# Norms between stages: gain on the rows, root in the turning diagonal, shift added in PSUM, splits of 512 columns, weight splits behind

## The reference

```
layers 0, 1:   x = layer_norm(ALPHA * x + mixer(x), g, b)
               x = layer_norm(ALPHA * x + conv_ffn(x), g, b)
layers 2, 3:   x = x + rmsnorm(mixer(rmsnorm(x, g0)), g1)
               x = x + rmsnorm(ffn(rmsnorm(x, g2)), g3)

layer_norm:    (x - mean) * rsqrt(var + 1e-5) * g + b      rows of 1024
rmsnorm:       x * rsqrt(mean(x*x) + 1e-6) * g
```

## Time and profile before

| | |
|---|---|
| median of 3 executions | 1635.89 us (1635.73 to 1636.53) |
| the profiled execution | 1639.12 us, span 1637.8 us |
| PE busy | 1476.4 us (90%), mean granted clock 0.936 |
| DVE busy | 989.1 us (60%) |
| ACT busy | 771.2 us (47%) |
| POOL busy | 348.8 us (21%) |
| DMA | 242.53 MB, 148 GB/s on average |

### The profile page before, as it was taken

How to read it: one execution, slowest core, us unless ns; L and a number is a source line. 1 busy time by engine, 2 the same in 40 slices (tenths; PEclk the granted TensorE clock), 3 DMA queues, 4 the chain that set the end, 5 groups by cost and what they waited for, 6 DMA issues and landing times.

```text
span 1637.8 us, 24046 instructions
## 1 busy us (share of the span) xinstructions
PE 1476.4 (90%) x9862; PEld 1318.7 (81%) x9862; DVE 989.1 (60%) x1721; ACT 771.2 (47%) x1168; POOL 348.8 (21%) x278
## 2 busy tenths in 40 slices
PE   7989987999989879999799989999897757989998
PEld 6888767999877769998666779999697755789997
DVE  5366447666638366676346265566579996265655
ACT  4343435455442255454444465444565553364443
POOL 0267132000177530001732410000100041500000
PEclk8999997999987979999899999999998976999999
DMA  7543223555344325654312335654442211335552
GB/s 267 223 167 116 103 77 129 184 206 190 141 148 155 129 103 185 227 180 155 134 73 91 114 118 183 215 180 155 180 155 104 104 53 64 129 136 199 193 184 74
DMA packets 37101, 242.53 MB, mean 148 GB/s; under 512 B 3928, under 2 KB 6272, under 8 KB 9472
## 3 DMA queue, kind: packets, MB, share of 16 engines
q1 hardware_dynamic: 36992, 241.00, 40.9%
HBM read 236.27 MB, written 4.72 MB: 147 GB/s over the span
## 4 chain that ended last, share of the span: by engine, by line
PE 74%; DVE 12%; ACT 7%; POOL 5%; issue 2%; DMA 0%; SPq 0%; ACTq 0%; DVEq 0%; POOLq 0%
PE ps L328 23%; PE ps L295 14%; PE ps L296 13%; PE ps L297 13%; POOL wlo L245 4%; DVE wlo L252 2%; ACT whi L237 2%; DVE gb L1938 1%; PE ps L1591 1%; PE ps L835 1%; PE ps L1605 1%; PE ps L426 1%; ACT gb L1847 1%; DVE ar L1975 1%; ACT XS L460 1%
## 5 line engine op out<-in xcount | busy, mean ns | idle before, releaser
L295 PE MATMUL ps<-XS,whi 128*128 128x256 f32 x2088 | 607.2, 291 | 28.5 <-DVE XS L480 18.1
L296 PE MATMUL ps<-XS,whi 128*128 128x256 f32 x2088 | 602.2, 288 | 0.0
L297 PE MATMUL ps<-XS,wlo 128*128 128x256 f32 x2088 | 601.6, 288 | 0.0
L252 DVE TENSOR_TENSOR wlo<-raw,whi 128x2048 fp32r<-128x2048 f32 x160 | 368.8, 2306 | 170.8 <-ACT whi L237 170.8
L237 ACT ACTIVATE whi<-raw 128x2048 fp32r<-128x2048 f32 x212 | 403.7, 1906 | 144.3 <-PE ps L328 132.1
L245 POOL TENSOR_TENSOR wlo<-raw,whi 128x512 fp32r<-128x512 f32 x206 | 275.3, 1369 | 827.2 <-ACT whi L237 827.2
L295 PEld LDWEIGHTS ps<-XS,whi 128*128 128x128 f32 x2088 | 412.9, 198 | 35.2 <-issue 24.6
L296 PEld LDWEIGHTS ps<-XS,whi 128*128 128x128 f32 x2088 | 412.6, 198 | 1.6 <-issue 0.2
L297 PEld LDWEIGHTS ps<-XS,wlo 128*128 128x128 f32 x2088 | 411.8, 197 | 0.0
L328 PE MATMUL ps<-whi,MS 128*128 128x512 f32 x1088 | 312.9, 393 | 12.1 <-POOL wlo L245 11.5
L328 PEld LDWEIGHTS ps<-whi,MS 128*128 128x128 f32 x1088 | 202.2, 189 | 55.2 <-POOL wlo L245 13.1
(11 more groups left out here) (264 smaller groups left out, 1590.7 us busy)
## 6 DMA issues: line engine op xcount, KB each, us to landing
raw<-in_up SPq DMA_DIRECT2D x88, 1024.0 KB, 4.8
raw<-in_down SPq DMA_DIRECT2D x44, 1024.0 KB, 4.8
raw<-in_hg_t SPq DMA_DIRECT2D x16, 1024.0 KB, 4.8
raw<-in_od_t SPq DMA_DIRECT2D x8, 1024.0 KB, 4.8
raw<-in_ev_a SPq DMA_DIRECT2D x7, 1024.0 KB, 5.1
raw<-in_wa_o SPq DMA_DIRECT2D x6, 1024.0 KB, 4.8
raw<-in_hg_o SPq DMA_DIRECT2D x6, 1024.0 KB, 4.8
raw<-in_mem_k SPq DMA_DIRECT2D x4, 1024.0 KB, 7.8
```

What stands on the lines that cost most here:

```text
L252: ve.tensor_tensor(lo[:, 0:w], r[:, 0:w], hi[:, 0:w].bitcast(F32), ALU.subtract).then_inc(w_lo_v)
L295: pe.matmul(d, hi[:, c], S[:, k, 0:256], start=(k == 0), stop=False)
L296: pe.matmul(d, hi[:, c], S[:, k, 256:512], start=False, stop=False)
L297: last = pe.matmul(d, lo[:, c], S[:, k, 0:256], start=False, stop=(k == 7))
```

## The change

- Norms 0 to 2: DVE multiplies the centred rows by the gain row in natural order (two operations of 512 columns, before the root is needed). The turn is an f32 matmul with a diagonal `dm` that holds the root. Ahead of each of its blocks stands a matmul with one row of contraction that writes the shift into PSUM (shift row against a row of ones), onto which the turn adds.
- Norms 3 to 6: DVE multiplies the new rows by the gain of the coming norm (`gp`, loaded by a new DMA from a DRAM copy that PE, ACT and SP make of the gain columns at norm 0), and these are turned; the order of the residual sum changes so that the multiplication by gb comes before the root.
- A turned bank holds four blocks: banks 4 and 5 for tt = 0, banks 2 and 3 (the accumulators just read) for tt = 1. ACT copies 512 columns a time to the high part, DVE subtracts 512 columns a time for the low part, of both row tiles. POOL splits none.
- The weight splits of tile `LAST[n] + 2` stand behind both row tiles on ACT and on DVE.
- The rows in natural order are made by DVE: `layer_rows_dve`, for norms 0 and 2 in the FFN at j = 2 and 4, for norm 1 at the start of the odd stage, for norm 3 in the norm. POOL has none left.
- SP no longer waits for the norm before it loads for the next stage, but for the last activations of the stage before. The squares on ACT go to the arena instead of yb. Two buffers of the even stage (QA, CN) share the place of QI and KI.

```diff
         def norm_pe(n):
+            if n == 0:
+                pe.transpose(bank[7][0:32, 0:128], pc[:, PC["rg"][0]:PC["rg"][1]], ident).then_inc(g_tp.up())
             for tt in range(2):
...
+                for q in range(2):
+                    o = turn_bank(tt, q)
+                    pe.wait_ge(ly.sem, 4 * n + 2 * tt + q + 1)
+                    pe.wait_ge(dg.sem, 2 * n + tt + 1)
+                    if n < 3:
+                        pe.wait_ge(d_gb, 16 * (n + 1))
+                    for i in range(4):
+                        k = 4 * q + i
+                        d = o[:, 128 * i:128 * i + 128]
                         if n < 3:
...
+                            pe.matmul(d, gb[0:1, 1, 128 * k:128 * k + 128], C("ones", 1)[:, 0:128], start=True, stop=False)
+                        last = pe.matmul(d, yb[:, tt, 128 * k:128 * k + 128], dm[:, tt, :], start=(n >= 3), stop=True)
                     last.then_inc(tp.up())
...
         def xs_act(n, tt):
...
+            for q in range(2):
+                hi, lo, bv = xs_views(tt, q)
+                ac.wait_ge(tp.sem, 4 * n + 2 * tt + q + 1)
+                ac.activation(hi, bv, ACT.Copy).then_inc(xh.up())
+
+        def xs_dve(n, tt):
+            for q in range(2):
+                hi, lo, bv = xs_views(tt, q)
+                ve.wait_ge(xh.sem, 4 * n + 2 * tt + q + 1)
+                ve.tensor_tensor(lo, bv, hi.bitcast(F32), ALU.subtract).then_inc((xs1 if tt else xs0).up())
...
             root_dve(st[:, o + 14:o + 15], st[:, o + 13:o + 14], 1.0, LN_EPS)
-            ve.tensor_scalar(yb[:, tt, :], yb[:, tt, :], st[:, o + 12:o + 13], st[:, o + 14:o + 15],
-                             ALU.subtract, ALU.mult).then_inc(ly.up())
+            ve.wait_ge(d_gb, 16 * (n + 1))
+            for h in range(2):
+                c = half_rows(h)
+                ins = ve.scalar_tensor_tensor(yb[:, tt, c], yb[:, tt, c], st[:, o + 12:o + 13], gb[:, 0, c], ALU.subtract,
+                                              ALU.mult)
+                ins.then_inc(ly.up() if n < 3 else dv.up())
+            meanwhile()
+            root_ready()
+
+        def diagonal_dve(tt, r):
+            ve.tensor_scalar(dm[:, tt, :], ident, r, None, ALU.mult).then_inc(dg.up())
+
+        def layer_rows_dve(n, tt):
+
+            o = 32 * tt
+            for h in range(2):
+                c = half_rows(h)
...
+                ve.scalar_tensor_tensor(xn[:, tt, c], yb[:, tt, c], st[:, o + 14:o + 15], gb[:, 1, c], ALU.mult,
+                                        ALU.add).then_inc(xr.up())
...
+        def residual_dve(n, tt):
+
+
+            def gained(h):
+                c = half_rows(h)
+                ve.tensor_tensor(yb[:, tt, c], accs[tt][h][:, :], gb[:, 0, c], ALU.mult).then_inc(dv.up())
+
+            ve.wait_ge(d_gb, 16 * (n + 1))
+            ve.wait_ge(sq.sem, got["sq"] + 1)
+            gained(0)
+            mean_square_dve(tt, 22)
+            gained(1)
+            root_ready()
+            ve.wait_ge(dv.sem, dv.n)
+            for h in range(2):
+                c = half_rows(h)
+                ve.wait_ge(xr.sem, xr_at(n - 1, tt, h))
+                ve.scalar_tensor_tensor(xn[:, tt, c], yb[:, tt, c], st[:, 32 * tt + 25:32 * tt + 26], xn[:, tt, c],
+                                        ALU.mult, ALU.add).then_inc(xr.up())
+
+        def gained_dve(n, tt):
+
+            ve.wait_ge(d_gp, 16 * (n - 2))
+            for h in range(2):
+                c = half_rows(h)
+                ve.wait_ge(xr.sem, xr_at(n, tt, h))
+                ve.tensor_tensor(yb[:, tt, c], xn[:, tt, c], gp[:, c], ALU.mult).then_inc(ly.up())
...
         def norm_dve(n):
             if n < 3:
                 layer_norm_dve(n, 0)
+                diagonal_dve(0, st[:, 14:15])
                 layer_norm_dve(n, 1)
-                dve_weights(LAST[n] + 2)
-                xs_dve(n)
+                diagonal_dve(1, st[:, 46:47])
...
+            xs_dve(n, 0)
+            xs_dve(n, 1)
+            dve_weights(LAST[n] + 2)
...
         def norm_act(n):
...
+            if n < 7:
+                xs_act(n, 0)
+                xs_act(n, 1)
+                act_weights(LAST[n] + 2)
...
+        def next_gain_sp(n):
+
+            if n == 3:
+                sp.wait_ge(g_cp.sem, 1)
+                sp.dma_start(pre.rearrange("n (k p) -> (n k) p", p=128), gp[0:32, 0:128]).then_inc(d_pre, 16)
+                sp.wait_ge(d_pre, 16)
+            else:
+                sp.wait_ge(ly.sem, 4 * n)
+            src = pre[n - 3]
+            sp.dma_start(gp[:, :], bass.AP(tensor=src.tensor, offset=src.offset, ap=[[0, 128], [1, 1024]])).then_inc(d_gp, 16)
...
                 if j % 2 and 0 < j // 2 < 9:
                     dve_weights(t + 4)
+                if k < 2 and j in (2, 4):
+                    layer_rows_dve(2 * k, j // 2 - 1)
...
         def odd_dve():
+            layer_rows_dve(1, 0)
+            layer_rows_dve(1, 1)
...
         def odd_pool():
-            stage_pool(ov, 1, oo + 4)
+            pool_weights(oo + 4)
```

More of the change, by code:

```diff
@@ L169, in program @@
         lb = sb("lb", [128, 48])
-        xf = [sb(f"xf{i}", [128, 256]) for i in range(4)]
+        gp = sb("gp", [128, 1024])
+        dm = sb("dm", [128, 2, 128])
         ar = sb("ar", [128, ARENA])
@@ L440, in xs_act @@
-        def xs_act(n, tt):
[L441 to L448, removed]
-                if tt == 0 or q % 2:
-                    ac.wait_ge(tp.sem, 8 * n + 4 * tt + q + 1)
-                    if tt:
-                        ac.wait_ge(xs0.sem, 4 * n + q + 1)
-                    ac.activation(xf[q][:, 0:128], bank[4 + q][:, 0:128], ACT.Identity, scale=gain(n, 2 * q),
-                                  bias=shift(n, 2 * q))
-                    ac.activation(xf[q][:, 128:256], bank[4 + q][:, 128:256], ACT.Identity, scale=gain(n, 2 * q + 1),
-                                  bias=shift(n, 2 * q + 1)).then_inc(aa.up())
-                    ac.wait_ge(aa.sem, aa.n)
-                else:
-                    ac.wait_ge(xe.sem, 2 * n + q // 2 + 1)
-                ac.activation(hi, xv, ACT.Copy).then_inc(xh.up())
@@ L577, in of_x @@
             def of_x(tt):
-                if n == 3 and tt == 0:
-                    waits = [(xn_p.sem, 15), (xn_p.sem, 16)]
-                else:
-                    waits = [(xr_v.sem, xr_at(n, tt, h)) for h in range(2)]
-                squares_act(tt, lambda h: xn[:, tt, 512 * h:512 * h + 512], 16, waits)
-            if n == 7:
-                of_acc(0)
-                of_acc(1)
-                return
+                squares_act(tt, lambda h: xn[:, tt, half_rows(h)], 16, [(xr.sem, xr_at(n, tt, h)) for h in range(2)])
+            if n == 0:
+                ac.wait_ge(g_tp.sem, 1)
+                ac.activation(gp[0:32, 0:128], bank[7][0:32, 0:128], ACT.Copy).then_inc(g_cp.up())
             if n == 3:
@@ L591, in norm_act @@
             elif n > 3:
-                of_acc(0)
-                of_x(0)
-                of_acc(1)
-            xs_act(n, 0)
-            if n > 3:
-                of_x(1)
-            act_weights(LAST[n] + 2)
-            xs_act(n, 1)
+                for tt in range(2):
+                    of_acc(tt)
+                    if n < 7:
+                        of_x(tt)
+            if n < 7:
+                xs_act(n, 0)
+                xs_act(n, 1)
+                act_weights(LAST[n] + 2)
@@ L1327, in ffn_dve @@
                     dve_weights(t + 4)
+                if k < 2 and j in (2, 4):
+                    layer_rows_dve(2 * k, j // 2 - 1)
             dve_weights(LAST[2 * k + 1] + 1)
-        def stage_pool(first, n, end):
-            for step in range(4):
-                pool_weights(first + 2 * step + 2)
-                rows_pool(n, step)
-            pool_weights(end)
         def ffn_pool(k):
-            if k < 2:
-                for step in range(4):
-                    rows_pool(2 * k, step)
             pool_weights(LAST[2 * k + 1] + 1)
```

200 lines of the change are left out of this document (64 added, 136 removed).

## The result

The changed kernel takes 1647.59 us (median of 8 runs, 1642.45 to 1648.30) against 1636.21 for the kernel before on the same chip (8 runs, 1634.85 to 1640.64): ratio 1.0054, 95% interval 1.0038 to 1.0070. It is slower by 0.5%, outside the range and on the other side of the forecast. Each kernel's runs fall on two levels some 5 us apart (the changed kernel's upper one at a mean granted clock of 0.934 to 0.935, its lower one at 0.938 to 0.939), so the seams are read from the profiled executions: span 1646.5 against 1637.8, 8.7 us more.

What follows compares the result with a forecast made beforehand. PE bounds the kernel (74% of the chain), with time won only where it waits or runs at its lower clock, at the norms' seams. 2.4 - 6.9 + 2.1 + 1.0 + 3.3 - 3.0 + 2.7 + 1.4 = 3.0 us: 1632.9, range 1617 to 1643.

Steps and rivals of the forecast that it cites:

- What comes: Turn at norms 0 to 2: 64 records a norm, at 0.16 us high clock and 0.27 low.
- Rival B: One-row matmuls at 0.18 us high, 0.31 low; norm 0's turn ends at 256.8; 1640, or 1643 us; chance 0.20.
- Rival C: Gains at norms 0, 2, 4, 6 (10.5 us) cancel losses at 1 and 5 (9.9); 1633 to 1639; chance 0.20.
- Which clock: Norm 0's turn: clock falls 4.5 us in, after 28 records, with 36 x 0.27 = 9.7 us following.
- Rival A: The clock stays up through the turn: 18.6 us won in all, 1617 us; chance 0.25, whole or in part.
- The weight splits cost nothing at 0, 2, 4 and 6: Late splits lie under the first projection (5.8 to 7.7 us); without that cover, 5.0 us lost each.
- Norm 1, the missing cover: PE waits for POOL's low part until 468.1: 9.6 us lost, 2.7 regained later, net -6.9 (bounds -0.5 and -11).
- Norm 5: First accumulation wants two tiles, both DVE's; low part at 1161.4 against 1159.18; -3.0 us (bounds -1 and -4).
- Norms 3, 4, 6 and 7: Time won at these norms: +1 us at 3, +3.3 at 4, +2.7 at 6, +1.4 at 7.
- Free edits: DVE's row operations hidden (3 us each uncovered), gain loads bounded 0 to 3 us once, other edits 0.5 at most.

Runs made afterwards that it cites:

- the grouped one: Changed kernel with the four one-row shift matmuls of a bank put first, then its four turns, the same work: 1620.04 us, ratio 0.9878 against the kernel before.

## Why the prediction was wrong

**The step that failed** is the price of the turn in "What comes": "I take 0.16 high, as the same width alternates there, and 0.27 low". Measured: 0.21 and 0.36 us a record. Both lie outside the bounds that I had set (0.18 and 0.31). The 0.16 came from the 40-row matmul of the earlier trace rows, whose weight load still overlaps because a 64-row matmul stands before it; only the matmul behind it has another load that waits. It paid for half a change where each matmul of the new turn pays for a whole one. The 128/8-row matmuls load 64 columns in place of 128. No row had a full-width one-row matmul next to a full one. Sixty-four records make 19.2 us of turn in place of 14.2. Put into the prediction's own sum this gives norm 0 -2.6, norm 1 -11.9 and norm 2 -2.9, within 1 us of the -1.8, -11.4 and -3.7 measured, and the whole sum becomes 12 us lost in place of 3.0 won, 1648 us. That this meets the measured 1647.6 is luck: the profile has only 5.3 us lost in the norms and stages, as norms 3 to 7 won 11.7 us in place of 5.4; 3.4 us of clock ahead of the first norm come on top, and the rest is that the profiled execution of the kernel before was 2.9 us above its median.

Rival B, "slower, through the one-row matmuls", named the mechanism and its side; its price was too low, so its 1640 to 1643 fell short too. Rival C needed gains at norms 0 and 2 to cancel the losses, and there were none.

**Point by point.**
- *Which clock*: right. Forecast to fall 4.5 us into the turn, measured 5.0, with PE busy. Rival A, in which it stays up, came about only once the rows were filled (64 or 128) or the shift matmuls left out. The Trainium skill, "TensorE: Matmul & The Clock Gate", section "Why this matters for your kernels", warns of long idle gaps between bursts. The gap of 3.2 us after which the clock fell agrees with it. The one of 2.3 us is shorter than the gap it warns of, and the clock fell all the same; the changed kernel's clock fell with no gap at all.
- *A reading that was wrong*: the earlier trace rows start at 253 and do not show that the clock fell in the idle gap ahead of it. It fell before that gap, at 245.7, while the last transposes ran and 1.6 us behind an idle gap of 2.94 us between the two halves (granted clock 1.00 from 244 to 245, 0.84 from 245 to 246, 0.50 from 246).
- *The weight splits cost nothing at 0, 2, 4 and 6*: right, no wait there. What I left unsaid is what moving them wins at norms 0 and 2: alone, in the kernel before, it took both seams from 13.2 to 6.6 us, some 2 us of which the stages behind gave back. The changed kernel without its shift matmuls has 6.3, so the other edits add little there.
- *Norm 1, the missing cover*: right. PE starts behind "POOL's four pieces", forecast 7.9 us after the turn (468.1 less 460.2), measured 9.45: DVE's rows beside them cost 1.9 us, not 0.3. The odd stage is 5.1 us shorter, not 2.7: 2.0 us are the two waits for POOL that went, the rest goes with the clock.
- *Norm 5*: the wait came as forecast (4.86 us behind DVE's low part), but the shorter seam ahead of it and 1.8 us in the stage behind it made up for it: +0.2 against -3.0.
- *Norms 3, 4, 6 and 7*: +11.5 in all against +8.4 (1.0 + 3.3 + 4.1), most of the surplus at norm 3 and the stage behind it, which I did not pull apart.
- *Free edits*: no new wait of PE or DVE for a gain load shows in the profile, and none of PE for rows in the feed-forward.
- 3.4 us of the profile's difference lie ahead of the first norm, where the two kernels are alike and the clock was low for 34.1 us in place of 27.3; no term of the sum could hold them.

## What to carry to other kernels

Price a small matmul by its neighbours: one that adds a constant row to PSUM was dear here beside matmuls of 128 rows (0.415 us each), and filled up to 128 rows it was not (0.22). A PE busy at 100% can be a PE at half its clock: read the step between starts and the granted clock, not the share. And where a prefetch stands relative to the critical copies is a choice for each stage: behind them where the next stage's first tiles are ready, ahead where that stage opens with the very tile.

## What the hardware showed that I had not expected

Each change between 128 rows and 1 or 64 in neighbouring f32 matmuls of 128 columns cost 0.20 us at 2.4 GHz (0.415 against 0.2225 us a matmul), and the weight load then started with its matmul and not 0.11 us ahead; from 64 to 40 rows it kept its lead. The granted clock fell about 5 us into a busy turn of alternating one-row and 128-row matmuls, some 8 us into the grouped one at norm 2, and not at all with 64 or 128 rows. And unchanged code ahead of the first norm differed by up to 9 us from kernel to kernel (237.4 to 246.3), with 20.5 to 37.5 us of it at 1.2 GHz; what sets those stretches is open.
